# Reordering the fills of the state-space loop: indexer keys earlier, the query factors before the last two key projections

## The reference, cut to what matters

```python
z = h @ w_in
u, q, k, v, qi, ki, wi = jnp.split(z, SPLITS, axis=-1)
q = rope(rmsnorm(q.reshape(B, L, N_HEADS, HEAD_DIM), q_norm), pos)
k = rope(rmsnorm(k.reshape(B, L, N_HEADS, HEAD_DIM), k_norm), pos)
qi = rope(qi.reshape(B, L, N_IDX_HEADS, IDX_DIM), pos)
ki = rope(ki[:, :, None, :], pos)[:, :, 0]
...
bu = jnp.einsum('blgc,gpc->blgp', ug.astype(jnp.complex64), b_bar)
a_cum, h = lax.associative_scan(combine, (a, bu), axis=1)
y = jnp.real(jnp.einsum('blgp,gcp->blgc', h, c_mat)) + d_skip.astype(f32).reshape(N_SSM_GROUPS, SSM_GROUP) * ug
```

## Time and profile before

| | |
|---|---|
| median of 3 runs | 1640.68 us (1637.76 to 1640.78) |
| the profiled execution | 1640.78 us |
| its span in the trace | 1638.9 us |
| PE busy | 1564.9 us (95%) |
| DVE busy | 1255.5 us (77%) |
| ACT busy | 981.4 us (60%) |
| POOL busy | 113.8 us (7%) |
| moved by DMA | 420.80 MB, mean 257 GB/s |

### The profile page before, as it was taken

One profiled execution on the slowest core, in us unless ns is written; L12 is line 12 of the kernel. 1 busy time (PEld: TensorE's weight loads), 2 busy tenths in 40 slices (PEclk: granted clock), 3 DMA queues, 4 the chain that ended last, 5 costly groups with the idle time before them and its releaser, 6 DMA issues.

```text
span 1638.9 us, 23592 instructions
## 1 busy us (share of the span) xinstructions
PE 1564.9 (95%) x7853; PEld 1267.7 (77%) x7853; DVE 1255.5 (77%) x1659; ACT 981.4 (60%) x1290; POOL 113.8 (7%) x156
## 2 busy tenths in 40 slices
PE   6998988899999579999999999999999999999998
PEld 5664554699999478888888888888888888888887
DVE  8978820255554679889989988888988988998986
ACT  5111442244443157777777777777777777777784
POOL 1377510000000000000000000000000000000000
PEclk9898979999999779999999999999999999999999
DMA  6401125334544419999989999998998998998992
GB/s 226 151 26 52 56 93 167 135 111 162 183 140 134 182 63 360 367 327 336 371 329 336 361 353 321 363 355 315 359 361 309 355 365 317 345 371 318 354 358 84
DMA packets 212887, 420.80 MB, mean 257 GB/s; under 512 B 10233, under 2 KB 56469, under 8 KB 212572
## 3 DMA queue, kind: packets, MB, share of 16 engines
q1 hardware_dynamic: 211542, 414.37, 70.3%
q10 hardware_dynamic: 622, 3.45, 0.5%
q0 software_dynamic: 672, 2.32, 0.4%
HBM read 417.50 MB, written 3.07 MB: 257 GB/s over the span
## 4 chain that ended last, share of the span: by engine, by line
PE 85%; DVE 3%; ACT 1%; issue 1%; DMA 1%; SPq 0%; ACTq 0%; DVEq 0%
PE bank L1252 19%; PE bank L1257 19%; PE bank L1256 19%; PE bank L1130 3%; PE bank L1133 3%; PE bank L1134 3%; PE bank L1207 2%; PE bank L1113 2%; PE bank L1277 1%; PE bank L1215 1%; PE bank L1145 1%; PE bank L1149 1%; PE bank L1148 1%; PE bank L860 1%; PE bank L823 1%
## 5 line engine op out<-in xcount | busy, mean ns | idle before, releaser
L2114 DVE TENSOR_TENSOR split<-raw_w,split 128x1024 fp32r<-128x1024 f32 x672 | 783.0, 1218 | 50.4 <-ACT split L1627 48.2
L1627 ACT ACTIVATE split<-raw_w 128x1024 fp32r<-128x1024 f32 x672 | 684.4, 1060 | 109.1 <-PE bank L1252 108.0
L1252 PE MATMUL bank<-split,xgr 128*128 128x512 f32 x896 | 359.2, 401 | 6.0 <-DVE split L2114 6.0
L1257 PE MATMUL bank<-split,xgr 128*128 128x512 f32 x896 | 354.4, 396 | 0.0
L1256 PE MATMUL bank<-split,xgr 128*128 128x512 f32 x896 | 354.2, 395 | 0.0
L1252 PEld LDWEIGHTS bank<-split,xgr 128*128 128x128 f32 x896 | 169.3, 189 | 43.8 <-DVE split L2114 6.4
L1257 PEld LDWEIGHTS bank<-split,xgr 128*128 128x128 f32 x896 | 169.1, 189 | 39.9
L1256 PEld LDWEIGHTS bank<-split,xgr 128*128 128x128 f32 x896 | 169.4, 189 | 37.5
L1252 PE MATMUL bank<-split,hbr 128*128 128x512 f32 x448 | 177.9, 397 | 0.0
L1257 PE MATMUL bank<-split,hbr 128*128 128x512 f32 x448 | 176.9, 395 | 0.0
L1256 PE MATMUL bank<-split,hbr 128*128 128x512 f32 x448 | 176.9, 395 | 0.0
(11 more groups left out here) (386 smaller groups left out, 1945.7 us busy)
## 6 DMA issues: line engine op xcount, KB each, us to landing
raw_w<-in_moe_gate SPq DMA_DIRECT2D x112, 1024.0 KB, 5.2
raw_w<-in_moe_up SPq DMA_DIRECT2D x112, 1024.0 KB, 5.9
raw_w<-in_moe_down SPq DMA_DIRECT2D x112, 1024.0 KB, 5.1
ring<-in_w_gate SPq DMA_DIRECT2D x11, 1024.0 KB, 5.0
ring<-in_w_up SPq DMA_DIRECT2D x11, 1024.0 KB, 7.3
ring<-in_w_down SPq DMA_DIRECT2D x8, 1408.0 KB, 6.4
ring<-in_w_in SPq DMA_DIRECT2D x5, 2048.0 KB, 9.5
ring<-in_w_out SPq DMA_DIRECT2D x2, 2048.0 KB, 8.1
```

The lines of the kernel that those rows point to most:

```text
L1252: first = mm(out, hi, place[:, s, 0, cols], start=start, stop=False)
L1257: last = mm(out, hi, place[:, s, 1, cols], start=False, stop=stop)
L1627: A(place[:, s, 0, :], raw_w[:, at:at + BLOCK], ACT.Copy).then_inc(sem("high_ready"), 1)
L2114: TT(place[:, s, 1, :], raw_w[:, at:at + BLOCK], place[:, s, 0, :].bitcast(F32), ALU.subtract).then_inc(sem("low_ready"), 1)
```

## The change

The groups from j = 5 on are rewritten. All fills stay, 88 of them up to the end of the loop, so all fills after the loop keep their banks. `("skT", 2)` to `("skT", 5)` come earlier. `("qe", c)` moves from group 10 to group 9, `("k", 2)` from 9 to 10 and `("k", 3)` from 10 to 11, beside `"kn"`. `("skT", 6)` moves from 11 to 10, and `("y", 2)` moves from group 14 to group 15, behind `("ke", c)`. Since a bank follows from the place in the list, the banks of the fills between change too.

```diff
@@ fill_order
     groups = [[], four("qis") + ["kis", "wiT"], [("q", 0), "wbd"], [("q", 1)] + keys(0), [("q", 2)] + keys(1),
-              [("q", 3), "qn"], four("qs") + keys(2), [("k", 0)] + keys(3), [("k", 1)] + keys(4), [("k", 2)] + keys(5),
-              four("qe") + [("k", 3)], ["kn"] + keys(6, 7), ["kidT", ("y", 0)], four("ks"), [("y", 1), ("y", 2)],
-              four("ke")]
+              [("q", 3), "qn"] + keys(2), four("qs") + keys(3), [("k", 0)] + keys(4), [("k", 1)], four("qe") + keys(5),
+              [("k", 2)] + keys(6), [("k", 3), "kn"] + keys(7), ["kidT", ("y", 0)], four("ks"), [("y", 1)],
+              four("ke") + [("y", 2)]]
     assert len(groups) == NJ
     for j, group in enumerate(groups):
         f += group + [("bur", j), ("bui", j)]
```

## The result

The changed kernel took 1652.57 us, the median of 4 runs (1651.25 to 1653.12), against 1640.73 us of 4 runs before. The ratio is 1.0074, with a 95% interval of 1.0057 to 1.0090. A second comparison, with 6 runs against 27, gave 1.0062 (1.0045 to 1.0079). So the change is slower, as forecast, but by 0.6 to 0.7% and not by the 0.35% that the prediction gave, and 1652.57 lies outside the range. From trace to trace the span grew by 11.8 us, from 1638.9 to 1650.7.

The account below looks back on a forecast made before the run. PE was taken to set the loop's pace up to tile 12's pair, DVE after it. 4.17 + 1.56 = 5.73 us on 1640.78 gave 1646.5 us, whole range 1641.5 to 1651; slower had chance 0.62.

Parts of the forecast that it names:

- Keys 2 and 3: Group 5: a key ahead of tile 5's pair starts tile 5 0.91 us later; PE reaches tile 8's pair as before.
- PE held by a bank: Tile 9's pair waits for DVE's last scan of tile 8 at 118.06, holding ("k", 2); pause of about 2 us.
- the 95.5 of the forecast: Sign in the changed kernel's trace: DVE's tile 5 starts near 95.5.
- `("k", 2)` and `kn`: PE before tile 12: ("k", 2) slow at 5.66 us; ("k", 3) to kn 4.92, with 0.88 of waiting.
- the term 4.17: PE's steps from 118.1 sum to 23.17 us, so tile 12's pair comes at 141.27 instead of 137.10.
- another 1.56 us: Loop's tail: y2 opens at 157.57, takes 6.18 us partly at the lower clock, and delays the last scan.
- The loop's end: DVE's last scan of the loop ends at 168.64, against 162.91 before.
- I take a loop that ends later by some time to make the whole later by that time: Stages behind the loop: they follow its end step by step, so the 5.73 us pass whole to the total.
- a later stage gives time back: Behind the loop, likely sample and attention between 210 and 290: faster, total about 1636 us; chance 0.06.
- The first rival: Clock stays high at ("k", 2) and y2 in the loop: only +2.5 us, 1643.3, within 0.2%; chance 0.24.
- the second: Bank no obstacle for PE at tile 9: 1640.0 us, or 1641.7 with the slow projection; chance 0.08.

Follow-up runs that it names:

- the delay of 2.8 us: Kernel before with two added DVE products on an unread tile after the loop's last scan, order of fills unchanged: 1646.10 us, ratio 1.0021.
- both mends: Changed kernel with ("k", 2) and the four qe exchanged and ("y", 2) back beside ("y", 1): 1649.25 us, ratio 1.0029.
- split `qe`: Changed kernel with ("qe", 0) and ("qe", 1) put beside ("k", 1), the other two left with key 5: 1652.22 us, ratio 1.0061.
- `y0` late: Kernel before with ("y", 0) moved from group 12 to the end of group 13, behind the four ks: 1643.82 us, ratio 1.0016.

## Why the prediction was right in direction and wrong in size

- **Keys 2 and 3.** Right. From the start of tile 4 to that of tile 5 it took 8.03 us before and 8.95 after, 0.9 longer. Tile 5 itself started 0.66 earlier, since the pair of tile 1 and `("q", 0)` met less of the lower clock in this execution (from that pair to the pair of tile 2 7.00 us instead of 8.65). The keys alone showed no difference.
- **PE held by a bank.** Right at the pair of tile 9, but incomplete. DVE went from the start of tile 5 to the end of tile 8 in 22.6 us in both kernels, so tile 8's bank came free at 116.53, the forecast 118.06 less the 1.6 by which tile 5 started before the 95.5 of the forecast, and the pair came at 116.67. The pause itself lay elsewhere: I had overlooked that `("qe", 2)` needs tile 7's bank. PE waited there for 1.75 us, and the slow `qe` and key 5 filled the rest. `("k", 0)` at the full clock gained nothing, since it only brought PE to its banks sooner. The exchange with `k2` gave back 2.4 us in one trace and nothing in another. (The kernel before did not have both banks of tile 7 under this pair, as I wrote: `("bui", 9)` took that of `("k", 1)`.)
- **`("k", 2)` and `kn`.** As priced: 5.64 us from start to start, against 5.66, and 4.92 against 4.92. The clock fell at 112 already, so the `qe`, key 5 and the pair before `k2` were slow too.
- **The pair of tile 12**, the term 4.17: 5.26 measured from tile 4 to tile 12. Of the 1.1 too little, 1.0 is the pair of tile 9, 2.13 us to the next fill at the lower clock instead of 1.14. Forecast was 141.27, measured 140.78; that this is so near is luck, since the early start hid 1.6.
- **The tail**, the term "another 1.56 us": mis-sized, 3.66 measured. I had `y2` open at 157.57, behind the skip term of `y1`. Before it, though, stand `("ke", 2)` and `("ke", 3)`, whose banks are those of tile 13. They began at 156.68 and took 2.12 us at the lower clock, so `y2` began at 158.80, 1.23 later, and 1.72 later counted from the pair of tile 12. It lasted 6.65 instead of 6.18 us. The late `y2` alone cost 2.83 on the kernel before, and putting it back gave 3.64.
- **The loop's end**: forecast 168.64, measured 170.25.
- **"I take a loop that ends later by some time to make the whole later by that time"**: this is the step that failed most. The loop ended 7.34 us later, the whole 11.8. The other 4.4 us lie in the stages behind it: 0.5 up to the first `v` projection, 3.5 up to the dense part and 0.5 after that. Passed on one for one, the 7.34 us would have given 1648.1, inside the range. The windows show the 3.5 as PE's clock, and the trace with the delay of 2.8 us showed that the order isn't needed for it. The 4.4 are the difference of two traces, though. The medians of the later comparison differ by 8.9 us, 1.6 more than the loop's 7.3, so how much of the 4.4 comes in every run is open. The rival "a later stage gives time back" had the right place and the wrong sign.
- **The first rival**, that the clock stays high, fell: `k2` and `y2` both met the lower level. So did the second, that PE is not held: it was, and with `k3` or the `qe` elsewhere it was held at other fills.

What stays open is what decides how much of the lower clock the later stages meet. In 14 traces the stretch had values from 152.9 to 159.9 us. All six traces of the changed order or a mend of it lie at 156.7 or above, but so do four of the other eight within 0.3. The changed kernel's ten runs all lie between 1651.25 and 1654.25, while the one with both mends had runs from 1643.70 to 1651.13 and the one with split `qe` from 1644.94 to 1654.03, so the order seems to bear on what a run can take. I have no rule that tells this from the list of fills.

## What to carry to other kernels

With banks given out in turn, the question for a reordered fill is not only what it needs but who held its bank seven fills earlier, and what of the other engines' work stands behind it in the queue; walk through that for every short fill, not only for the pair that looks critical. A fill that can't open holds all behind it, and where it is long, as `y2`, it must not come between the last wait and the last tile. And a stage's gain or loss is not the kernel's: in its trace the version with `y0` late had gained 3.9 us by the end of the loop, and all of it was gone at the end, 4.0 of it in the stretch where PE's clock was 0.90 instead of 0.93.

## What the runs showed of the hardware

The kernel before, unchanged, spread over 13 us in 85 runs beside the experiments (on three chips, with nearly the same range on each), and the time went with the mean granted clock of the run:

| mean granted clock | 0.964 | 0.965 | 0.966 | 0.967 | 0.968 | 0.969 | 0.970 | 0.971 | 0.972 | 0.973 |
|---|---|---|---|---|---|---|---|---|---|---|
| runs | 2 | 9 | 13 | 20 | 12 | 10 | 8 | 2 | 6 | 3 |
| mean time, us | 1646.6 | 1646.8 | 1644.3 | 1644.2 | 1641.4 | 1641.5 | 1638.9 | 1638.9 | 1636.3 | 1634.7 |

That is about 1.4 us for each 0.001, in steps of some 2.6 us rather than evenly. The changed kernel's runs were at 0.963 to 0.966. Its six at 0.965 took 1652.1 us on average, 5.3 more than the kernel before at the same value. I had taken the spread for noise of the measurement and the clock for a property of each matmul's neighbourhood. In this kernel it is a term of the total, of the same size as the change.

The clock fell at 120.8 in the kernel before, where PE had been busy throughout, so a busy PE alone did not keep it high. In the changed kernel it fell in the pause of 1.75 us behind 111.0, after 13.1 us in which PE was busy throughout. These two traces have a fall with a pause and one without.
